# A three-layer transformer on one Trainium2 core: feature banks, late norms, tile-wise boundaries between layers, and the last level of a triangular inverse

## Time and profile before

| what | value |
|---|---|
| median of 3 runs | 2936.47 us (2935.63 to 2937.44) |
| the profiled execution | 2936.3 us |
| its span in the profile | 2934.5 us |
| TensorE matmuls busy | 2874.2 us, 98% |
| VectorE busy | 1658.2 us, 57% |
| ScalarE busy | 1392.3 us, 47% |
| chain that ended last, share of L492 (granules) on TensorE | 87% |
| weights and inputs read | 511.76 MB, 175 GB/s over the span |

### The profile page before, as it was taken

One profiled execution on the slowest core, in us unless ns is written; L12 is line 12 of the kernel. 1 busy time (PEld: TensorE's weight loads), 2 busy tenths in 40 slices (PEclk: granted clock), 3 DMA queues, 4 the chain that ended last, 5 costly groups with the idle time before them and its releaser, 6 DMA issues.

```text
span 2934.5 us, 37445 instructions
## 1 busy us (share of the span) xinstructions
PE 2874.2 (98%) x15082; PEld 2383.3 (81%) x15082; DVE 1658.2 (57%) x2078; ACT 1392.3 (47%) x1788; POOL 25.2 (1%) x43
## 2 busy tenths in 40 slices
PE   8999999999999999999999999999999999999998
PEld 7888877788888888878887878888888887888886
DVE  5786865554544454564445554554454567776655
ACT  5554465544444444454446454444444445455444
POOL 0000000000000000000000000000000000000000
PEclk9999999999999999999999999999999999999999
DMA  6543345556555555555552655565565654444553
GB/s 239 173 152 107 122 137 188 177 189 196 184 190 198 188 187 192 194 172 187 188 187 71 208 189 189 185 199 187 190 197 186 202 185 148 140 158 167 195 173 129
DMA packets 255846, 516.84 MB, mean 176 GB/s; under 512 B 8528, under 2 KB 8752, under 8 KB 254688
## 3 DMA queue, kind: packets, MB, share of 16 engines
q1 hardware_dynamic: 252896, 501.61, 51.9%
q0 software_dynamic: 2816, 13.33, 1.4%
HBM read 511.76 MB, written 2.10 MB: 175 GB/s over the span
## 4 chain that ended last, share of the span: by engine, by line
PE 96%; DVE 2%; ACT 1%; issue 1%; DMA 0%; SPq 0%; ACTq 0%; DVEq 0%
PE acc L492 87%; PE side L560 1%; PE side L697 1%; PE side L690 1%; ACT ar L1167 1%; PE side L826 1%; PE side L588 0%; DMA raw<-in_ev_w_in 0%; PE side L970 0%; PE side L1010 0%; PE side L979 0%; PE side L1029 0%; DVE ar L1887 0%; PE side L1118 0%; DVE ar L1890 0%
## 5 line engine op out<-in xcount | busy, mean ns | idle before, releaser
L1899 DVE TENSOR_TENSOR wlo<-raw,whi 128x1024 fp32r<-128x1024 f32 x948 | 1155.0, 1224 | 1076.5 <-ACT whi L1178 1075.1
L1178 ACT ACTIVATE whi<-raw 128x1024 fp32r<-128x1024 f32 x948 | 999.0, 1060 | 1157.9 <-PE acc L492 1157.5
L492 PE MATMUL acc<-whi,xh 128*128 128x512 f32 x3008 | 824.5, 396 | 4.8 <-ACT whi L1178 4.4
L492 PE MATMUL acc<-wlo,xh 128*128 128x512 f32 x3008 | 807.3, 390 | 0.3
L492 PE MATMUL acc<-whi,xl 128*128 128x512 f32 x3008 | 807.0, 390 | 0.0
L492 PEld LDWEIGHTS acc<-wlo,xh 128*128 128x128 f32 x3008 | 565.6, 188 | 121.4 <-DVE wlo L1899 2.9
L492 PEld LDWEIGHTS acc<-whi,xl 128*128 128x128 f32 x3008 | 566.2, 188 | 120.1
L492 PEld LDWEIGHTS acc<-whi,xh 128*128 128x128 f32 x3008 | 555.7, 189 | 116.4 <-issue 5.7
L492 PE MATMUL acc<-whi,hTh 128*128 128x512 f32 x784 | 212.0, 392 | 0.0
L492 PE MATMUL acc<-wlo,hTh 128*128 128x512 f32 x784 | 209.7, 389 | 0.1
L492 PE MATMUL acc<-whi,hTl 128*128 128x512 f32 x784 | 209.7, 389 | 0.0
(11 more groups left out here) (269 smaller groups left out, 1268.2 us busy)
## 6 DMA issues: line engine op xcount, KB each, us to landing
raw<-in_ffn_w_gate SPq DMA_DIRECT2D x88, 1024.0 KB, 5.1
raw<-in_ffn_w_up SPq DMA_DIRECT2D x88, 1024.0 KB, 5.2
raw<-in_ffn_w_down SPq DMA_DIRECT2D x88, 1024.0 KB, 5.0
raw<-in_ev_w_in SPq DMA_DIRECT2D x56, 1024.0 KB, 5.1
raw<-in_od_w_in SPq DMA_DIRECT2D x48, 1024.0 KB, 5.1
raw<-in_w_in SPq DMA_DIRECT2D x32, 1024.0 KB, 5.3
raw<-in_ev_w_out SPq DMA_DIRECT2D x16, 1024.0 KB, 5.0
raw<-in_od_w_out SPq DMA_DIRECT2D x16, 1024.0 KB, 5.0
```

What stands on the lines that cost most here:

```text
L492: mm = pe.matmul(acc[2 * pair + t][:], x[:, k0 + j, t * P:t * P + P], w[:, ring, j], start=start and j == 0, stop=stop and j == 1)
L1178: act.activation(whi[:, place % RING], raw_granule(place), ACT.Copy).then_inc(S("hi_done"), 1)
L1899: dve.tensor_tensor(wlo[:, place % RING], raw_granule(place), whi[:, place % RING].bitcast(F32), ALU.subtract).then_inc(S("lo_done"), 1)
```

## The change

1. **Banks.** The rounds of `ev_out` use banks 3, 0, 1, 0, 1, 0, 1, 0; in `z_aside` TensorE turns a round before the stick-breaking stage, and ScalarE and VectorE take rounds 0 and 1 behind the first two splits of `ev_out`, before their stages.
2. **Late norms.** `o_root(1, t)` and the table preload move on ScalarE behind the first split of `ev_z`, `gdn_norm(1, t, True)` on VectorE behind its first and second.
3. **Boundaries by tile.** The last two granules of the last chunk ahead of a boundary run all of tile 0 and then all of tile 1 (`by_tile`); sum, square, root, reciprocal and additions run tile by tile; the first two rounds are turned tile by tile (`open_stream`), the other six in pairs before granules 1, 2 and 3. The `lead` comes behind the second split instead of the third.
4. **Last level.** One 64 by 64 product per head for each of the two products, a copy of a quarter of T, no mask for level 6, a subtraction on one block; `gated_values` takes the mask's place at level 5.
5. Semaphore counts follow; `ab_copied` is folded into `ab_done`; `expand_b(0, ...)` in `s_in` moves from places 3, 4, 5 to 4, 5, 6.

```diff
+STREAM_AT = {1: (2, 3), 2: (4, 5), 3: (6, 7)}
+STREAM_READY = (3, 4, 6, 8)
+def feature_bank(name, i):
+    return (3, 0, 1, 0, 1, 0, 1, 0)[i] if name == "ev_out" else i % 4
...
 (TensorE, granules)
+                        if name in POST and c == CHUNKS[name] - 1 and j >= per - 2:
+                            if j == per - 1:
+                                by_tile(name, pair, lhs_h, lhs_l)
+                            yield
+                            continue
+            def by_tile(name, pair, lhs_h, lhs_l):
...
+                for t in range(TT):
+                    for n in range(2):
+                        g = gran(name, CHUNKS[name] - 1, per - 2 + n)
+                        if t == 0:
+                            pe.wait_ge(S("hi_done"), g + 1)
+                        sweep(n, t, lhs_h, whi)
+                        sweep(n, t, lhs_l, whi)
+                        if t == 0:
+                            pe.wait_ge(S("lo_done"), g + 1)
+                        mm = sweep(n, t, lhs_h, wlo, stop=n == 1)
+                        if t:
+                            mm.then_inc(S("used"), 1)
+                        elif n:
+                            mm.then_inc(S("tile_done"), 1)
...
+            def open_stream(name, src):
+                n = ("up0a", "od_in", "up1a", "s_in").index(name)
+                base = 8 * TOF[name]
+                banks = [claim(side[r], "xl_done", 2 * (base + r) + 2) for r in range(2)]
+                for t in range(TT):
+                    pe.wait_ge(S("h_done"), 8 * n + (STREAM_READY[0] if t else 1))
+                    for k in range(4):
+                        mm = pe.transpose(banks[k // 2][:, k % 2 * TOK + t * P:k % 2 * TOK + t * P + P],
+                                          src[:, t, k * P:k * P + P], ident)
+                        if t and k % 2:
+                            mm.then_inc(S("tof_ready"), 1)
...
 (TensorE, last level)
+                    if l < 6:
+                        mm = mm4_halves(b, lambda k: U(LM_)[:, k], lambda k: U(M_)[:, k])
+                    else:
+                        for k in range(4):
+                            mm = pe.matmul(b[64:128, k * P:k * P + 64], U(LT_)[0:64, k, 64:128], U(M_)[0:64, k, 0:64],
+                                           start=True, stop=True)
...
             def z_aside(c, j):
+                if c == 1 and j > 5:
+                    to_features("ev_out", u, (j - 6,))
                 if j % 2:
                     sb_stage(4 * c + j // 2)
-                if c == 1 and j > 5:
-                    to_features("ev_out", u, (j - 6,))
...
 (ScalarE)
-            for t in range(TT):
-                o_root(1, t)
...
             def z_aside(c, j):
+                if (c, j) == (0, 0):
+                    for t in range(TT):
+                        o_root(1, t)
+                    act.preload_act_table_set("natural_log_exp_and_others")
...
+            def roots_out(name, user):
+                before_root()
+                for t in range(TT):
+                    square_out(name, 3, (t,))
+                    act.wait_ge(S("ssum_done"), 2 * POST[name] + t + 1)
+                    if POST[name]:
+                        act.wait_ge(S("rstdu_done"), 2 * POST[name] + t - 1)
+                    run(rms_u[:, t:t + 1], ssum[:, t:t + 1], ACT.Sqrt, "rmsu_done", scale=1.0 / DM, bias=EPS)
+                features_hi(user, range(2))
...
 (VectorE, into_stream; root sums and reduces, scale takes the reciprocal, add adds one piece into h)
+                root(0)
+                gained(name, 3, (0,))
+                scale(0)
                 if n == 0:
                     dve.wait_ge(S("x_back"), 16)
+                add(0, 0)
+                add(0, 1)
+                root(1)
+                scale(1)
+                add(1, 0)
+                add(1, 1)
+                gained(name, 3, (1,))
+                features_lo(user, range(2))
+                def rest(j):
+                    if j in (2, 3):
+                        add(0, j)
+                        add(1, j)
+                    if j - 1 in STREAM_AT:
+                        features_lo(user, STREAM_AT[j - 1])
+                return rest
...
 (VectorE, level 6)
-                        gated_values(t)
                         dve.wait_ge(S("p_ready"), ready + 1)
-                        tt(unit(t, MT_), unit(t, MT_), four(side[2 + t][:]), sub, inv)
+                        x = unit(t, MT_)[0:64, :, 64:128]
+                        tt(x, x, four(side[2 + t][:])[0:64, :, 64:128], sub, inv)
```

More of the change, by code:

```diff
@@ L759, in _ @@
+                    if l < 6:
+                        mm = mm4_halves(b, lambda k: U(T_)[:, k], lambda k: U(MT_)[:, k])
+                    else:
+                        for k in range(4):
+                            mm = pe.matmul(b[0:64, k * P + 64:k * P + 128], U(T_)[64:128, k, 0:64],
+                                           U(MT_)[64:128, k, 64:128], start=True, stop=True)
+                    mm.then_inc(S("p_ready"), 1)
                 for n in range(13):
@@ L1182, in linear, with granules @@
                     pass
-            def granules(name, evac, lead, aside=None, after=2):
+            def granules(name, evac, lead, aside=None, after=2, lead_at=None):
                 per = KTS[name] // 2
@@ L1191, in granules @@
                         split(gran(name, c, j))
-                        if j == min(after, per - 1):
-                            if c == 0:
-                                lead()
-                            else:
-                                evac(c - 1)
+                        if c == 0 and j == min(after if lead_at is None else lead_at, per - 1):
+                            lead()
+                        if c and j == min(after, per - 1):
+                            evac(c - 1)
                         if aside:
@@ L1719, in s_aside @@
             def s_aside(c, j):
+                if c == 0 and j - 1 in STREAM_AT:
+                    features_hi("s_in", STREAM_AT[j - 1])
                 at_ = 8 * c + j
@@ L2218, in z_aside @@
             def z_aside(c, j):
+                if c == 0 and j < 2:
+                    gdn_norm(1, j, True)
                 if j % 2 and 8 * c + j > 1:
@@ L2229, in _, with summed, gained @@
             linear("ev_z", z_gate, lambda: None, z_aside)
-            def gained(name, c):
+            def summed(name, c, t):
+                pair = (CHUNK0[name] + c) % 2
+                x = u[:, t, c * CH:c * CH + CH]
+                if c == 3 and t == 0:
+                    dve.wait_ge(S("tile_done"), POST[name] + 1)
+                else:
+                    chunk_done(name, c)
+                dve.wait_ge(S("half_done"), 8 * (int(name[2]) + 1))
+                tt(x, acc[2 * pair + t][:], x, ALU.add, "u_done")
+            def gained(name, c, tiles=range(TT)):
                 n = POST[name]
@@ L2239, in gained @@
                 cl = slice(c * CH, c * CH + CH)
-                if name[:2] == "dn":
-                    l = int(name[2])
-                    chunk_done(name, c)
-                    dve.wait_ge(S("half_done"), 8 * (l + 1))
-                    for t in range(TT):
-                        tt(u[:, t, cl], acc[2 * pair + t][:], u[:, t, cl], ALU.add, "u_done")
-                for t in range(TT):
+                if name[:2] == "dn" and c < 3:
+                    for t in tiles:
+                        summed(name, c, t)
+                for t in tiles:
                     dve.wait_ge(S("sq_done"), 8 * n + 2 * c + t + 1)
@@ new lines, in scale, with add @@
+                def scale(t):
+                    dve.wait_ge(S("rmsu_done"), 2 * n + t + 1)
+                    dve.reciprocal(rstd_u[:, t:t + 1], rms_u[:, t:t + 1]).then_inc(S("rstdu_done"), 1)
+                    dve.wait_ge(S("rstdu_done"), 2 * n + t + 1)
+                def add(t, c):
+                    cl = slice(c * CH, c * CH + CH)
+                    dve.wait_ge(S("ug_done"), 8 * n + 2 * c + t + 1)
+                    stt(h[:, t, cl], u[:, t, cl], rstd_u[:, t:t + 1], h[:, t, cl], ALU.mult, ALU.add, "h_done")
@@ L2306, in block_of @@
                             split(i * 16 + (g0 + 8 * m + j), j)
+                            if m == 0 and first and j == (1 if rest else 2):
+                                lead()
+                            if m == 0 and first and rest and j > 1:
+                                rest(j)
                             if m == 0 and j == 2:
-                                if first:
-                                    lead()
-                                else:
+                                if not first:
                                     dve.wait_ge(S("used"), i * 16 + g0)
@@ L2660, in s_aside @@
             def s_aside(c, j):
+                if c == 0 and j > 1:
+                    later[0](j)
                 at_ = 8 * c + j
```

197 lines of the change are left out of this document (97 added, 100 removed).

## The result

The changed kernel took 2917.07 us (median of 4 runs, 2916.56 to 2917.85), the kernel before 2936.05 us beside it (2933.72 to 2937.44): a ratio of 0.9937, 95% interval 0.9922 to 0.9953. 19.0 us are gone, 18.9 were predicted. The sum is right; the sizes of its terms are not all, and four differences of 0.4 to 1.8 us cancel. The interval of the ratio is 4.5 us wide on either side, so the agreement within 0.1 us is luck.

The account below looks back on a forecast made before the run. TensorE, busy 98% of the span, bounds the kernel, so only its idle and half-speed time can be won, besides work taken from it. 6.2 + 4.4 + 5.5 + 2.8 = 18.9 us off 2936.3 gave about 2917.5, range 2909.5 to 2923.5.

Parts of the forecast that it names:

- Boundaries: Four layer boundaries: granule 3 sooner after E (TensorE's end), 12.8 us at full clock, 6.2 us after 6.6 for half clock.
- The wait for h: Sign at the boundaries: TensorE's wait at L560 falls from 18.8 us to below 10, in more and shorter pieces.
- E+16 and E+14.5: Sign at the boundaries: where granule 3 stands after TensorE's end E, behind down and output projections.
- The clock's share: Half clock after boundary gaps: 2.3 us behind a down projection, 1.0 behind an output projection, 6.6 us in sum.
- rival (a): The clock stays at 2.4 GHz over all boundaries: 6.6 us more gained, 2910.9 us; chance 0.14.
- Rival (b): Clock falls at every boundary and returns later, another slow stretch behind down projections: 12.2 instead of 6.6, 2923.0 us; chance 0.17.
- Late norms: Start of ev_z: the wait for the high split and granule 0's half clock go, 4.4 us saved.
- Banks: First features of ev_out: waits of 0.57 and 3.31 us and the slow granule behind them go, 5.5 us saved.
- Rival (c): Roots in ev_z or the gate product hold TensorE as before: 4.4 us or so back, 2921.9 us; chance 0.10.
- The last level: Inverse's last level: single-block products at 0.54 us per four, 0.1 of waiting; 1.4 us saved per head group, 2.8 for two.
- VectorE's slack: Granules behind each boundary: VectorE needs 11.5 us against TensorE's 10.6; about 1.1 us of slack left, costed at nothing.
- Rival (d): Features of the three later rounds become serial, 7.1 us a step against 3.5: 43 us added, 2960 us; chance 0.03.

Follow-up runs that it names:

- fifth run: Changed kernel with the last two granules ahead of each boundary in the old matmul order, chain still tile by tile: 2935.06 us.
- filled kernel: Changed kernel with TensorE multiplying the identity by itself, into a bank nobody reads, in the gaps of the four boundaries: 2910.79 us.
- early sum and cut row: Changed kernel with tile 1's sum ahead of tile 0's second addition at down projections, and kernel_base's 128-product rows cut into halves of 64: 2914.32 us.
- early-sum kernel: Changed kernel with VectorE's sum of tile 1 at the down projections put ahead of tile 0's second addition into h: 2920.07 us.

## Why the prediction was right

**Boundaries: right, in the chain and nearly in the clock.** The working put granule 0 at E+5.75 and E+3.8 and, at full clock, granule 3 at E+16.3 and E+14.4. Measured were 5.3 and 3.6, and with filled gaps 16.2 and 14.6. The order by tile carries it, as the fifth run shows. Undone, the boundaries cost 6.2 us, the very term, but that is partly luck: the two profiles differ by 6.6 us up to granule 3, by 0.8 in s_in, and by falls of the clock elsewhere. Two of the signs were missed. The wait for h came to 10.1 us, just not below 10. "E+16 and E+14.5" for granule 3 leaves out the prediction's own clock term; with it they would be E+18.6 and E+15.4, and 17.6 to 17.85 and 16.1 to 16.4 were measured.

**The clock's share: right in sum, wrong in its two halves.** 2.3 us were charged behind a down projection and 1.0 behind an output projection; the profile has 1.6 at three and 1.3 at s_in (4.45, 4.47, 4.43 and 4.19 less 2.86), 6.1 in all for 6.6. The two errors are 1.7 too much and 1.2 too little, and that they nearly cancel is luck. The single size is not a constant either. Over the seven profiled kernels that have the tile-wise boundaries unfilled, granule 0 was slow behind all 14 gaps of 4.7 to 5.5 us at down projections (a cost of 1.3 to 1.6 us in eight, of 2.4 in six) and behind 8 of the 14 gaps of 3.6 to 3.9 us at output projections, with 2.86 to 2.88 at the other six. So 2.3 is the size of the longer falls, which this profile happens not to have, and 1.0 is near the mean of 0 and 1.6, but no execution has it. Filling the gaps gave 6.3 us, so the rival (a) was a possible kernel, only not this one, and 2910.79 was measured for its 2910.9. Rival (b) fell: the clock did fall at every boundary of the profiled execution, but for a shorter time than before behind down projections, and no further slow stretch followed (granules 1 and 2 take 2.8 us each with their clock at 1.00). The Trainium skill ("TensorE: Matmul & The Clock Gate", Part 1: The HAM clock gate) says that the throttled state is the default, which activity lifts; the filled kernel agrees (2.85 with products in the gap, 4.45 with idle). Six of the 14 shorter gaps, though, were not followed by half clock, and the falls of the last section come in rows where the records show TensorE busy; the rule as it is worded does not tell of these, and the measurement decides. The same section says of a kernel's start that how much of it is slow varies from run to run; up0a here shows such a variation from one kernel's profile to the next, in the middle of the kernel (4.45 us in the changed kernel's, 2.88 with the banks undone).

**Late norms: right.** 4.4 us were predicted and found, the wait and the half clock together. Undone they cost 5.3 in the median, 4.4 of it at this place.

**Banks: right in mechanism, 0.6 too small.** The wait of 3.31, the 0.57 before it and the slow granule have gone; the rest is smaller waits around them, for which no row stood in the sum. Rival (c), the roots or the gate product holding TensorE, did not occur.

**The last level: the term that was mis-sized.** 1.4 per head group was predicted. A group of four single products took 0.61 us (254.55 to 255.16), where 0.54 was taken, which is a small miss. The larger one is "0.1 of waiting": the second product of unit 1 waits 0.72 us for ScalarE's copy of T, which the shorter products no longer cover. That makes 0.96 in head group 0. In head group 1 the level saves 1.58 us at full clock, where 1.4 was predicted: from 345.57 to 353.89, 8.32 us, in the profile with early sum and cut row, against 9.90 before (346.97 to 356.87). But in the changed kernel's profile the shorter, gappier level is followed by half clock, which takes all of it: 9.92 us from 345.37 to 355.29. The prediction asked for the clock at the boundaries alone, not where its own shortening opened gaps. Part 4 was worth 1.9 us in the median, of the 2.8. Taking the double of the paired price came near: 0.61 us for a group of single products against 0.27 for as many paired instructions.

**VectorE's slack.** Costed at nothing, and no wait for late low splits or additions appeared in granules 1 to 3, which follow at 3.6 us. In s_in 1.0 us came on top behind granule 3 that was not in the sum. Of it 0.8 lies ahead of `kernel_base`: before, the low weights of three granules come late (the split of the one at 2456.30 ends at 2457.43, its sweep starts at 2457.48), and each of these granules takes 3.14 instead of 2.72 us; after, only one does (2445.84 to 2448.98), and with the boundaries undone three do again. The prediction saw these splits late and let the moved expansions cost nothing; it didn't ask what the new order would give back. Whether the move of the expansions or the rest of the boundary's order does it was not separated. Rival (d), serial rounds, has no trace.

## What to carry to other kernels

Where a chain of norm and additions stands between two maps, let the last granules end one tile first: the chain then starts half a granule pair early, and without that lead splitting the chain brings nothing (granule 3 at E+21.2 behind a down projection, against E+19.4 with the chain unsplit). Price the clock with every gap that a change leaves or opens, shortened products among them, and if it falls, fill the gap with products that nobody reads, counted from a measured duration (0.24 us each here) and kept below the gap. When a variant that should win loses with a wide spread, compare the position of landmarks first: the loss may lie in a stretch that the edit doesn't touch.

## What was not expected of the hardware

The clock also falls while TensorE works without a gap, as far as the records show it. In a row of 128 products of 64 by 64 by 16, which the records show as busy all the time, the granted clock goes to half in some executions and not in others. These two windows are of the early-sum kernel (all engines, then granted clock, DMA share, GB/s):

```profile
2450.00:2454.00 4.00, 4.00 (x81) 3.40 (x81) 3.96 (x8) 4.00 (x7) 0.93 (x2) 1.00 0.26 50
2454.00:2458.00 4.00, 4.00 (x65) 3.76 (x63) 3.97 (x6) 1.64 (x3) 3.28 (x7) 0.57 1.04 325
```

Each such fall takes 1.6 or 3.1 us, and they account for the last column of the table: 480.0 without one (480.8 and 481.0 with the old boundaries, for the low splits), 481.5 with a fall of 1.6, 484.7 with 1.6 and 3.1, 486.1 with two of 3.1. They also explain the 6.2 us by which the kernel without the order by tile was slower than its boundaries. The three kernels with two halves of 64 products and a granule between had no fall there in their profiles, and their 5, 5 and 4 runs lie within 2.0, 0.6 and 1.6 us of each other. Of the eleven profiles with uncut rows four have no fall there either (before, changed, boundaries undone, last level undone), so three clean profiles alone could be chance (4/11 three times over, an estimate of one in twenty); against it speaks that the spread of the early sum fell from 8.4 to 2.0 us. Why a row falls in one execution and not in the next is open. The busy share of the records doesn't tell it, and shifting the row by 2 us goes with a change from none to two (changed kernel and early sum), but that single comparison shows no rule. It also isn't settled why the clock was low at 350 us in some kernels and not in others whose level was the same.
